# A decoder trunk on one core: 36 first-stage products, the expert selection, 40 products woven with the gate table, 96 ahead

## The reference

```
q = (h @ wq).reshape(b, t, PEER_HEADS, 2, PEER_HALF)            # 8 heads, two halves
s = einsum('bthpd,phnd->bthpn', q, sub_keys)                    # 128 keys for each half
sv, si = top_k(s, 16)
cand = (sv[..., 0, :, None] + sv[..., 1, None, :])              # 16 x 16 candidates
cv, ci = top_k(cand, 16)
e1 = take_along_axis(si[..., 0, :], ci // 16);  e2 = take_along_axis(si[..., 1, :], ci % 16)
gate = softmax(cv)                                              # 8 x 16 experts for each token
act = gelu(einsum('td,ted->te', h, u_tab[e1 * 128 + e2]))
y = einsum('te,ted->td', gate * act, v_tab[e1 * 128 + e2])
```

## Time and profile before

| | us |
|---|---|
| median of 3 runs | 2723.41 (2722.73 to 2725.99) |
| the profiled execution | 2724.56 |
| its span, first to last instruction | 2722.8 |
| PE matmul busy in it | 2549.7 (94%) |
| DVE / ACT / POOL busy | 1637.5 / 1334.7 / 936.9 |

### The profile page before, as it was taken

The page is one execution under the profiler, slowest core; times in us unless marked ns, Lnnn a source line. Parts: engine busy times, 40 slices in busy tenths (PEclk is TensorE's granted clock), DMA queues, the critical chain, the costliest instruction groups (busy, mean ns, idle before and its releaser), DMA issues.

```text
span 2722.8 us, 50873 instructions
## 1 busy us (share of the span) xinstructions
PE 2549.7 (94%) x17658; PEld 2380.3 (87%) x17658; DVE 1637.5 (60%) x3315; ACT 1334.7 (49%) x2008; POOL 936.9 (34%) x372
## 2 busy tenths in 40 slices
PE   6999889999889999999989998989998899999997
PEld 5989889899789999888779998989988899998886
DVE  6465621594896555577674556126939955556776
ACT  4565444455444444455444654444544444444554
POOL 4865665689000000000147666557960000000001
PEclk9999999999999999999999998999999999999999
DMA  5433443455456666677634344434545566666774
GB/s 182 155 132 120 159 156 130 135 166 191 150 196 223 205 217 200 224 239 245 211 119 163 132 148 139 140 124 155 183 148 187 193 225 213 209 216 224 239 239 147
DMA packets 186422, 488.66 MB, mean 179 GB/s; under 512 B 14384, under 2 KB 80944, under 8 KB 181296
## 3 DMA queue, kind: packets, MB, share of 16 engines
q1 hardware_dynamic: 179664, 445.88, 49.9%
q10 hardware_dynamic: 6624, 41.16, 4.0%
HBM read 452.38 MB, written 34.60 MB: 179 GB/s over the span
## 4 chain that ended last, share of the span: by engine, by line
PE 81%; DVE 9%; issue 3%; ACT 3%; POOL 2%; DVEq 0%; ACTq 0%; DMA 0%; SPq 0%; POOLq 0%
PE banks L759 25%; PE banks L430 16%; PE banks L432 15%; PE banks L431 15%; PE banks L738 3%; POOL w_lo L366 2%; PE banks L578 1%; DVE arena L1538 1%; DVE arena L1537 1%; DVE h_r L1231 1%; ACT w_hi L791 1%; PE banks L688 1%; PE banks L406 1%; PE banks L659 1%; PE banks L640 1%
## 5 line engine op out<-in xcount | busy, mean ns | idle before, releaser
L366 POOL TENSOR_TENSOR w_lo<-ring,w_hi 128x1024 fp32r<-128x1024 f32 x368 | 936.6, 2561 | 1768.9 <-ACT w_hi L791 1768.5
L791 ACT ACTIVATE w_hi<-ring 128x1024 fp32r<-128x1024 f32 x780 | 820.8, 1055 | 432.6 <-PE banks L759 337.5
L430 PE MATMUL banks<-h_r,w_hi 128*128 128x256 f32 x3408 | 983.0, 288 | 26.3 <-DVE h_r L1231 25.3
L431 PE MATMUL banks<-h_r,w_hi 128*128 128x256 f32 x3408 | 970.8, 285 | 0.0
L432 PE MATMUL banks<-h_r,w_lo 128*128 128x256 f32 x3408 | 970.4, 285 | 0.0
L430 PEld LDWEIGHTS banks<-h_r,w_hi 128*128 128x128 f32 x3408 | 660.1, 194 | 36.0 <-DVE h_r L1231 28.9
L431 PEld LDWEIGHTS banks<-h_r,w_hi 128*128 128x128 f32 x3408 | 660.7, 194 | 4.2 <-issue 0.5
L432 PEld LDWEIGHTS banks<-h_r,w_lo 128*128 128x128 f32 x3408 | 660.0, 194 | 0.0
L759 PE MATMUL banks<-w_hi,o_r 128*128 128x512 f32 x2048 | 565.9, 390 | 3.6 <-DVE o_r L1567 3.6
L1545 DVE TENSOR_TENSOR w_lo<-ring,w_hi 128x1024 fp32r<-128x1024 f32 x412 | 502.1, 1219 | 28.9 <-ACT w_hi L791 28.8
L759 PEld LDWEIGHTS banks<-w_hi,o_r 128*128 128x128 f32 x2048 | 378.0, 188 | 78.6 <-DVE o_r L1567 5.3
(11 more groups left out here) (238 smaller groups left out, 2534.7 us busy)
## 6 DMA issues: line engine op xcount, KB each, us to landing
ring<-in_stream SPq DMA_DIRECT2D x780, 512.0 KB, 3.3
gates_dram<-arena ACTq DMA_DIRECT2D x32, 1024.0 KB, 5.4
arena<-gates_dram SPq DMA_DIRECT2D x32, 1024.0 KB, 7.3
arena<-in_mem ACTq DMA_DIRECT2D x2, 1024.0 KB, 5.7
arena<-in_keys ACTq DMA_DIRECT2D x2, 1024.0 KB, 4.9
arena<-in_c_decay ACTq DMA_DIRECT2D x2, 768.0 KB, 7.0
x<-in_x SPq DMA_DIRECT2D x1, 1024.0 KB, 4.8
arena<-in_mem SPq DMA_DIRECT2D x1, 1024.0 KB, 6.8
```

The lines of the kernel that those rows point to most:

```text
L366: pool.tensor_tensor(w_lo[:, s, :], ring[:, s, :], w_hi[:, s, :], ALU.subtract).then_inc(sem(f"low{s}"), 1)
L430: pe.matmul(out, lhs[0], rhs[0], start=first, stop=False)
L431: pe.matmul(out, lhs[0], rhs[1], start=False, stop=False)
L791: act.activation(w_hi[:, s, :], ring[:, s, :], ACT.Copy).then_inc(sem(f"high{s}"), 1)
```

## The change

`AHEAD` goes from 80 to 96, so that the main part has 32 pairs and the tail 96 `down`. 36 products stand alone (`PURE` 9 groups), then come the transposes of the first half of tokens, one product, the transposes of the second half, one product. The woven part has two halves of 20 products, and the 32 batches of a half are dealt to the first 18 of them. Behind it come the zeroing of the four banks and 18 products alone.

On ScalarE the exponential stands behind the 32nd GELU, and each copy to `selT` is followed by one GELU. On VectorE the waits for the exponential and the division are put between side 0 and side 1 of the second half of tokens; `selected` is given once there for the first half of tokens, and once behind side 1 for the second. `one_hots` makes the first index's rows of four tokens with one TENSOR_TENSOR of 128x512 in place of four TENSOR_SCALARs. GpSimd makes the low parts of all four slots of group `G_AHEAD + PURE`, and VectorE those from the next group on. The transposes use PSUM banks 0 and 1 in place of 6 and 7. `stage` and `gate_tiles` move to a plain float32 view (`o_f`) of the branch buffer, and `sel` moves inside `arena`.

```diff
--- before.py
+++ after.py
@@ -32,15 +32,16 @@
 NK = 128
 SLOTS = 4
 
-AHEAD = 80
+AHEAD = 96
 BATCH = 4
 CHUNK = 16
 CHUNKS = T // CHUNK
 BATCHES = T // BATCH
 GB = 8
-PURE = 12
+PURE = 9
 MIXED = 2
-WOVEN = 12
+ALONE = PURE * SLOTS + 2
+WOVEN = 20
 TURN = 2 * AHEAD - NK
 
 
@@ -139,7 +140,9 @@
         w_lo = sb("w_lo", [P, SLOTS, D], F32R)
 
         h_r = sb("h_r", [P, 2, KC, T], F32R)
-        o_r = sb("o_r", [P, 6144], F32R)
+        with nc.sbuf_tensor("o_r", [P, 6144], F32R) as o_r:
+            pass
+        o_f = sb("o_f", [P, 6144])
         freq = sb("freq", [P, 2])
         ident = sb("ident", [P, P])
         iota = sb("iota", [P, P], BF16)
@@ -241,14 +244,14 @@
         best = part(23808, NT, PH, 2, TOPK)
         idx = part(24320, NT, PH, 2, TOPK, dt=U32)
         idxb = part(24832, NT, PH, 2, TOPK, dt=BF16)
-        sel = part(25088, NT, 3, P)
+        sel = part(22784, NT, 3, P)
 
         selT = part(26624, 3, T)
         one1 = part(24576, 2, BATCH, P)
         one2 = part(25600, 2, BATCH, P)
-        stage = part(20480, 2, NK, CHUNK)
-
-        gate_tiles = part(20480, 2, CHUNKS, GB, CHUNK)
+        stage = part(1024, 2, NK, CHUNK, of=o_f)
+
+        gate_tiles = part(1024, 2, CHUNKS, GB, CHUNK, of=o_f)
         y_rows = part(0, NT, D)
         product = part(24576, T)
 
@@ -273,7 +276,7 @@
         def batches_of(q):
 
             n = BATCHES // MIXED
-            return range(q * n // WOVEN, (q + 1) * n // WOVEN)
+            return range(min(n, q * n // (WOVEN - 2)), min(n, (q + 1) * n // (WOVEN - 2)))
 
         def bc(ap, axis, n):
             s = list(ap.shape)
@@ -369,11 +372,9 @@
             for s in range(SLOTS):
                 low_part(0, s)
             with pool.Fori(0, DEPTH) as l:
-                with pool.Fori(1, G_AHEAD + PURE) as g:
+                with pool.Fori(1, G_AHEAD + PURE + 1) as g:
                     for s in range(SLOTS):
                         low_part(l * GROUPS + g, s)
-                low_part(l * GROUPS + G_AHEAD + PURE, 0)
-                low_part(l * GROUPS + G_AHEAD + PURE, 1)
 
                 for s in range(SLOTS):
                     low_part(l * GROUPS + GROUPS, s)
@@ -719,15 +720,17 @@
                 settle()
                 with pe.Fori(0, PURE) as i:
                     up_group(i)
-                ev("selected", NT, NT)
+
+                def selection_turn(t):
+                    ev("selected", t + 1, NT)
+                    for n in range(3):
+                        m = pe.transpose(bank[:, t, n * P:(n + 1) * P], sel[:, t, n, :], ident[:, :])
+                    m.then_inc(sem("sel_turned"), 1)
+
+                ev("keys_out", 6, 4)
                 for t in range(NT):
-                    for n in range(3):
-                        m = pe.transpose(bank[:, 6 + t, n * P:(n + 1) * P], sel[:, t, n, :], ident[:, :])
-                    m.then_inc(sem("sel_turned"), 1)
-
-                ev("keys_out", 6, 4)
-                for b in range(4):
-                    pe.matmul(bank[:, b, :], zeros[:, :], bc(zeros[:, :], 1, 4), start=True, stop=True)
+                    selection_turn(t)
+                    up(G_AHEAD + PURE, t, PURE * SLOTS + t, t)
 
                 def spread(j, parity):
 
@@ -739,16 +742,18 @@
                                       start=True, stop=True)
                     m.then_inc(sem("spread"), 1)
 
-                ev("sel_turned_out", 2, 2)
                 settle()
                 with pe.Fori(0, MIXED) as i:
                     for q in range(WOVEN):
                         for j in batches_of(q):
                             spread(i * (BATCHES // MIXED) + j, j % 2)
-                        up(G_AHEAD + PURE + q // SLOTS + i * (WOVEN // SLOTS), q % SLOTS, PURE * SLOTS + q + i * WOVEN, q)
-                settle()
-                with pe.Fori(PURE + MIXED * WOVEN // SLOTS, AHEAD // SLOTS) as i:
-                    up_group(i)
+                        up(G_AHEAD + PURE + (q + 2) // SLOTS + i * (WOVEN // SLOTS), (q + 2) % SLOTS,
+                           ALONE + q + i * WOVEN, q)
+                ev("sel_turned_out", 2, 2)
+                for b in range(4):
+                    pe.matmul(bank[:, b, :], zeros[:, :], bc(zeros[:, :], 1, 4), start=True, stop=True)
+                for q in range(ALONE + MIXED * WOVEN, AHEAD):
+                    up(G_AHEAD + q // SLOTS, q % SLOTS, q, q)
 
                 def down(g, s, n, parity):
                     wait_tile(g, s)
@@ -1085,19 +1090,18 @@
                     for s in range(SLOTS):
                         gelu(G_AHEAD + i, s, s, i * SLOTS + s)
 
-                with act.Fori(0, 10) as i:
-                    gelu_group(i)
-
-                ev("keys_read", 6, 4)
-                with act.Fori(10, PURE) as i:
+                with act.Fori(0, PURE - 1) as i:
                     gelu_group(i)
                 ev("cand_max", NT, NT)
                 act.activation(cbest, cbest, ACT.Exp).then_inc(sem("cand_exp"), 1)
+                gelu_group(PURE - 1)
                 for t in range(NT):
                     ev("sel_turned", t + 1, 2)
                     act.activation(selT[:, :, t * P:(t + 1) * P],
-                                   bank[:, 6 + t, 0:3 * P].rearrange("p (a t) -> p a t", a=3),
+                                   bank[:, t, 0:3 * P].rearrange("p (a t) -> p a t", a=3),
                                    ACT.Copy).then_inc(sem("sel_turned_out"), 1)
+                    gelu(G_AHEAD + PURE, t, t, PURE * SLOTS + t)
+                ev("keys_read", 6, 4)
 
                 def spread_out(j, parity, chunk, at):
 
@@ -1119,9 +1123,10 @@
                                 act.wait_ge(sem("spread_free"), l * BATCHES + i * (BATCHES // MIXED) + j + 3)
                                 act.dma_start(a["gates"][bass.ds(i * (CHUNKS // MIXED) + j // per_chunk, 1)].rearrange(
                                     "c p b t -> (c p) b t"), chunk).then_inc(kept, 16)
-                        gelu(G_AHEAD + PURE + q // SLOTS + i * (WOVEN // SLOTS), q % SLOTS, q, PURE * SLOTS + q + i * WOVEN)
-                with act.Fori(PURE + MIXED * WOVEN // SLOTS, AHEAD // SLOTS) as i:
-                    gelu_group(i)
+                        gelu(G_AHEAD + PURE + (q + 2) // SLOTS + i * (WOVEN // SLOTS), (q + 2) % SLOTS, q,
+                             ALONE + q + i * WOVEN)
+                for q in range(ALONE + MIXED * WOVEN, AHEAD):
+                    gelu(G_AHEAD + q // SLOTS, q % SLOTS, q, q)
 
                 def gated_high(m, parity):
                     act.wait_ge(sem("multiplied"), l * NK + m + 1)
@@ -1518,23 +1523,22 @@
                         hot4 = hot.rearrange("p (h k) i -> p h k i", h=PH)
                         link(dve.tensor_tensor(hot4, hot4, bc(idxb[:, t, :, side, :], 2, TOPK), ALU.mult))
                         link(dve.tensor_reduce(sel[:, t, side, :], hot, AX.X, ALU.add))
-                ev("cand_exp")
-                link(dve.tensor_reduce(gsum, cbest, AX.X, ALU.add))
-                link(dve.reciprocal(gsum, gsum))
-                for t in range(NT):
-                    dve.tensor_tensor(sel[:, t, 2, :].rearrange("p (h k) -> p h k", h=PH), cbest[:, t],
-                                      bc(gsum[:, t], 2, TOPK), ALU.mult).then_inc(sem("selected"), 1)
-
-
-                ev("sel_turned_out", 2, 2)
+                        if t == NT - 1:
+                            if side == 0:
+                                ev("cand_exp")
+                                link(dve.tensor_reduce(gsum, cbest, AX.X, ALU.add))
+                                link(dve.reciprocal(gsum, gsum))
+                            dve.tensor_tensor(sel[:, side, 2, :].rearrange("p (h k) -> p h k", h=PH), cbest[:, side],
+                                              bc(gsum[:, side], 2, TOPK), ALU.mult).then_inc(sem("selected"), 1)
 
                 def one_hots(j, parity):
 
 
                     dve.wait_ge(sem("spread"), l * BATCHES + j + 1)
+                    dve.tensor_tensor(one1[:, parity], bc(iota_f[:, :], 1, BATCH),
+                                      bc(selT[:, 0, bass.ds(j * BATCH, BATCH)], 2, P), ALU.is_equal)
                     for t in range(BATCH):
                         at = bass.ds(j * BATCH + t, 1)
-                        dve.tensor_scalar(one1[:, parity, t, :], iota_f[:, :], selT[:, 0, at], None, ALU.is_equal)
                         ins = dve.tensor_scalar(one2[:, parity, t, :], iota_f[:, :], selT[:, 1, at], selT[:, 2, at],
                                                 ALU.is_equal, ALU.mult)
                     ins.then_inc(sem("hot_ready"), 1)
@@ -1547,10 +1551,11 @@
 
                 settle()
                 with dve.Fori(0, MIXED) as i:
+                    dve.wait_ge(sem("sel_turned_out"), l * NT + i + 1)
                     for q in range(WOVEN):
                         for j in batches_of(q):
                             one_hots(i * (BATCHES // MIXED) + j, j % 2)
```

(22 more changed lines are left out.)

1 line of the change is left out of this document (removed).

## The result

| us | before | changed |
|---|---|---|
| median (runs) | 2724.51 (4) | 2659.49 (4; 2656.66 to 2662.89) |
| profiled execution, span | 2724.56, 2722.8 | 2660.43, 2658.6 |

The ratio is 0.9763, with a 95% interval of 0.9749 to 0.9778: 65 us less. The forecast was 2658.

A forecast was written before the change was run, and what follows sets the result against it. TensorE, its matmuls busy for 94%, was taken as the bound, losing time in the woven part and at the selection. Per layer +12.6 - 46.4 + 0.6 = -33.2 us, -66.4 from 2724.56: 2658.2, forecast 2658, range 2648 to 2691.

The forecast's parts named there:

- the third batch of a place: Woven part before: it waits 1.13 us for one-hots, then runs alone; 16 places, 21.6 us lost per layer.
- the order on ScalarE: Selection before: VectorE waited 38.26 us for the exponential, behind the 48th GELU; the gap lost 9.4 us per layer.
- Step 1: ScalarE: exponential behind the 32nd GELU costs 0, hidden by one product; by the skill's page TensorE loses 1.7 us per layer.
- Step 2: VectorE's new order at the selection: `selected` 1 at 638.3, `selected` 2 near 648.7; side 1 takes 10.1 us.
- Step 3: TensorE's order at the selection: `selected` 2 is there by 0.2 us, no wait taken, 2 us as bad end.
- rival B: Selection is the new wait: 2 to 5 us per layer, 2662 to 2672; chance 0.10 for over 3 us in all.
- Step 4: Woven part: no third-batch waits; TensorE sets the pace, 4.55 us per place against VectorE's 4.05; merged operation 0.69 us.
- The sum: Per layer: first `down` +12.6, main part and tail -46.4, 0.6 us left for drains: -33.2; both layers -66.4.
- step 6: AHEAD 96: main part loses 16 pairs at 5.62 us, tail gains 16 `down` at 2.72: -46.4 us.
- A: VectorE or the DMA paces the woven part: 2691 with the merged operation at 1.13 us, 2676 by DMA; chance 0.15.
- C: Woven part: a slow merged one-hot operation makes the kernel slower, 2838 if it takes 2.29 us; chance 0.04.
- D: Woven part's waits aren't from the third batch and return; only the selection's gap goes, 9.4 us per layer: 2705; chance 0.04.

The follow-up runs named there:

- e1: Changed kernel with the 32 batches of a half dealt to the first 12 of its 20 products in place of the first 18: 2704.79 us.
- e4: Kernel before with only the exponential moved, behind the 32nd GELU in place of the 48th: 2712.03 us.
- e3: Changed kernel with the exponential behind the 36th GELU in place of the 32nd: 2670.74 us, ratio 0.9810.
- e2: Changed kernel with the merged one-hot operation undone, four TENSOR_SCALARs in place of one TENSOR_TENSOR: 2661.35 us, ratio to before 0.9776.
- e13: Kernel before with the merged one-hot operation alone: 2719.96 us, ratio 0.9978.
- e6: Changed kernel with VectorE's loop over the two halves of the woven part written out, without the jump back: 2655.11 us.
- e8: Changed kernel with the second half's transposes one product later and batches dealt to products 2 to 19 of 20: 2650.67 us, ratio 0.9733.

## Why the prediction was right

**The number and the signs.** The main mechanism held, but several of its terms did not, and three of the forecast's own signs of being wrong came. It named waits for `selected` over 1 us as wrong: 1.63 us. It named no wait for the one-hots over 0.5 us as right: there are 1.65 and 1.8. And it was to fall if a period with two batches isn't 4.76 us: it is 4.66. What follows says where each belongs.

**The bound and the two losses.** Both causes that the forecast named are confirmed by undoing them: the third batch of a place (e1, 22 to 24 us per layer) and the order on ScalarE (e4, 4.8 of 9.4 us alone; e3, 5.0 us for a delay of 11.4). The merged operation is worth 1.5 to 2.5 us here, AHEAD nothing that these runs tell. The single edits of e1, e4 and e2 add up to 28 to 32 of the 32.7 us; that they may be added, one of them taken in the other kernel, no run shows.

**Step 1, the exponential.** Right. It stands at 637.92, 0.42 us long, and the next GELU at 639.65. On ScalarE, in order of time:

```profile
636.62 1.28 ACT L1096 ACT_TABLE_LOAD   x1
637.92 0.42 ACT L1096 ACTIVATE arena<-arena 128x256 f32<-128x256 f32 x1
638.36 1.28 ACT L1084 ACT_TABLE_LOAD   x1
639.65 0.39 ACT L1084 ACTIVATE arena<-banks 128x256 f32<-128x256 f32 x1
```

From the start of each load to what follows it are 1.30 and 1.29 us. The drain by which the Trainium skill (ScalarE: Activation LUTs, "What ACT_TABLE_LOAD costs") would have added 1.7 us per layer isn't there; TensorE doesn't wait at this place.

**Step 2, VectorE.** Wrong in a term, small in effect. With the first product at 1.16 us later than in layer 0 of before, `selected` 2 was due at 649.9 and came at 651.4. I priced the two score products L1531 at 0.3 us; they took 1.96 and 2.39 beside GpSimd. L1522 beside GpSimd took 2.28 us, not 4.43, which gave 2.15 of these 3.7 us back; this was luck, since it hung on which of the two engines came first. I had said that GpSimd's last low part ends about where the one-hots begin and priced nothing for it; the first merged operation was held up to 2.87 us.

**Step 3, the margin of 0.2 us.** It wasn't there: TensorE waited 1.6 us for `selected` and 0.4 for the first one-hots. It is rival B's mechanism, below its size of 2 us; the clock didn't fall (1.00 in the row from 645 to 653).

**Step 4, the woven part.** No place with two batches waits. The merged operation took 0.69 us, 0.60 from start to start, as the line through two rows gave. The other rule of the Trainium skill (VectorE: DVE Perf Modes, "Mode 2×_2P"), one element a cycle for two tensors, thus cost nothing here. But two terms were off. `spread` and product in the changed kernel, in order of time on TensorE:

```profile
708.65 1.95 PE L741 MATMUL banks<-arena 128*128 128x128 f32 x16
...
713.32 1.05 PE L741 MATMUL banks<-arena 128*128 128x128 f32 x8
...
717.08 1.95 PE L741 MATMUL banks<-arena 128*128 128x128 f32 x16
...
721.74 1.95 PE L741 MATMUL banks<-arena 128*128 128x128 f32 x16
```

The period is 4.66 with two batches (717.08 to 721.74) and 3.76 with one, so a batch costs 0.89, not 0.94: I took the 4.76 of the kernel before for free of waits, since the profile showed none, and e13 shows that it wasn't. That made the sum 64 x 0.05 = 3.2 us per layer too high. And I wrote that the loops' heads were hidden, with one batch due: the table loads were, VectorE's jump, for which I had no term, wasn't (1.7 us, e6).

**The sum.** Per layer I had +13.2 for the first `down`, with the 0.6 us kept for turns. Batches -3.2, waits 1.6 + 0.4 + 1.7 - 0.6 = +3.1: 13.1 against 13.4 measured. The two errors cancelled; either alone would have moved the forecast by 6 us. That the forecast lies within 2 us of the measured time is therefore luck; the gain of some 65 us isn't. The prices of step 6 held to the hundredth (5.62, 2.72), and 66 us of stage gain answer 64.1 us between the two profiled executions. The other 2 us lie outside the sum; no run shows where they come from.

**The rivals.** A: VectorE had 12% to spare, and e2 shows that even the old form leaves TensorE ahead. The DMA moved 219 GB/s where I had 217, and no engine waited for it there. C and D fall with the 0.69 us and with e1.

## What to carry to other kernels

Look at the worst place of an interleaving, not at the sum of work: with two buffers a third item in one place waits, whatever the average is. An engine's times before a change hold its neighbours' interference; when a step moves to another moment, price it with and without the neighbour. A product of independent work put behind a hand-over hides what is late by less than its length, a loop's jump too.

## What the runs showed of the hardware that was not expected

- VectorE's operations with two inputs waited about 2.1 us each beside GpSimd's subtractions, and the trace shows the wait as busy time (1.23 us becomes 3.32). Where both began at once, GpSimd's took 4.55 us instead of 2.4.
- At its jump back over a body of 20 products' worth of work VectorE stood idle for 2.91 us, against 1.40 us in the kernel before, whose body has 12. Whether the length of the body makes the difference no run shows.
- Two executions can differ by the clock where the code is the same. Behind the cross-attention's norm of layer 1 TensorE waits 3.1 us in both of two profiled executions. In one the granted clock falls, in the other it doesn't. The wait, and the row of the 10 us around it, for the changed kernel:

```profile
PE banks L431 <- ACT arena L861: 3.1, 1, 3.1
```

```profile
1687.00:1697.00 10.00, 7.76 (x43) 7.76 (x44) 1.90 (x6) 4.84 (x9) 5.54 (x3) 0.66 0.54 178
```

and that row for e8:

```profile
1677.80:1687.80 10.00, 7.78 (x65) 7.78 (x66) 1.88 (x5) 6.15 (x11) 6.81 (x3) 1.00 0.54 180
```

From the sum of squares to the scores this stretch took 43.9 us in one and 41.4 in the other, in code that is the same. Therefore the distances above were compared and not only the whole times; part of the 8.8 us between e8's median and the changed kernel's can be this.
